# Dilated attention on one core: both slots of a pair per step in two row tiles, scores in full float without a split, values turned once in the projection

## The reference, cut to what matters

```python
q, k, v = parts of h @ w_in                     # q: 3 groups x 8 slots x 64; k, v: 8 slots x 64
for g, (window, dilation) in enumerate(((128, 1), (512, 4), (2048, 16))):
    # tokens by residue t % dilation; blocks of 128 queries against 256 keys (their own block and the one before)
    scores = (q_block @ k_blocks.T) * 64 ** -0.5, masked to 0 <= distance <= 128
    m = max(scores); p = exp(scores - m); den = sum(p)
    o[g] = (p @ v_blocks) / den;  lse[g] = m + log(den)
out = sum over g of softmax(lse)[g] * o[g]
y_attn = out * silu(g_attn)
```

## Time and profile before

| | us |
|---|---|
| median of 3 runs | 2815.51 (2813.55 to 2815.75) |
| the profiled execution | 2818.68 |
| its span | 2817.1 |
| PE busy | 2741.9 (97%) |
| PE weight loads | 2262.5 (80%) |
| DVE busy | 1591.9 (57%) |
| ACT busy | 1238.4 (44%) |
| POOL busy | 1573.7 (56%) |

### The profile page before, as it was taken

One profiled execution on the slowest core, in us unless ns is written; L12 is line 12 of the kernel. 1 busy time (PEld: TensorE's weight loads), 2 busy tenths in 40 slices (PEclk: granted clock), 3 DMA queues, 4 the chain that ended last, 5 costly groups with the idle time before them and its releaser, 6 DMA issues. The chain is left out here.

```text
span 2817.1 us, 45199 instructions
## 1 busy us (share of the span) xinstructions
PE 2741.9 (97%) x16510; PEld 2262.5 (80%) x16510; DVE 1591.9 (57%) x2527; ACT 1238.4 (44%) x2258; POOL 1573.7 (56%) x1078
## 2 busy tenths in 40 slices
PE   6999999999999999999999999999999999999998
PEld 5888888888887788888887777777999877788787
DVE  6335324797544345885534556565777786743433
ACT  5232233433234444332233655656777854532332
POOL 7777778877776788777774545544111354232000
PEclk8999999999999999999999999999999999999999
DMA  3557435532225255332135655545676578954543
GB/s 127 141 176 214 137 117 153 146 111 96 67 90 194 90 160 156 105 113 82 55 110 172 190 161 185 185 158 184 204 211 192 146 243 271 300 171 149 179 141 112
DMA packets 462813, 436.24 MB, mean 155 GB/s; under 512 B 60736, under 2 KB 403008, under 8 KB 454976
## 3 DMA queue, kind: packets, MB, share of 16 engines
q1 hardware_dynamic: 460352, 425.79, 48.8%
q0 software_dynamic: 2304, 8.39, 0.8%
HBM read 290.99 MB, written 143.13 MB: 154 GB/s over the span
## 5 line engine op out<-in xcount | busy, mean ns | idle before, releaser
L552 PE MATMUL p_acc<-h_kept,w_hi 128*128 128x512 f32 x1216 | 475.7, 391 | 4.6 <-ACT work L598 3.1
L554 PE MATMUL p_acc<-h_kept,w_lo 128*128 128x512 f32 x1216 | 474.1, 390 | 0.0
L553 PE MATMUL p_acc<-h_kept,w_hi 128*128 128x512 f32 x1216 | 474.1, 390 | 0.0
L433 POOL TENSOR_TENSOR w_lo<-p_sums,w_hi 128x512 fp32r<-128x512 f32 x300 | 387.2, 1307 | 131.8 <-ACT w_hi L639 131.8
L639 ACT ACTIVATE w_hi<-p_sums 128x512 fp32r<-128x512 f32 x300 | 189.2, 632 | 472.6 <-PE p_acc L554 447.9
L552 PEld LDWEIGHTS p_acc<-h_kept,w_hi 128*128 128x128 f32 x1216 | 228.8, 188 | 54.4 <-ACT work L598 3.3
L554 PEld LDWEIGHTS p_acc<-h_kept,w_lo 128*128 128x128 f32 x1216 | 228.8, 188 | 47.8
L553 PEld LDWEIGHTS p_acc<-h_kept,w_hi 128*128 128x128 f32 x1216 | 228.9, 188 | 47.0
L552 PE MATMUL p_acc<-p_ops,w_hi 128*128 128x512 f32 x608 | 238.0, 391 | 7.1 <-DVE p_ops L740 7.1
L553 PE MATMUL p_acc<-p_ops,w_hi 128*128 128x512 f32 x608 | 237.3, 390 | 0.0
L554 PE MATMUL p_acc<-p_ops,w_lo 128*128 128x512 f32 x608 | 237.3, 390 | 0.0
(11 more groups left out here) (344 smaller groups left out, 6686.7 us busy)
## 6 DMA issues: line engine op xcount, KB each, us to landing
raw<-w_in SPq DMA_DIRECT2D x100, 512.0 KB, 4.7
s_qs<-p_stage SPq DMA_DIRECT2D x96, 256.0 KB, 4.0
work<-s_gates SPq DMA_DIRECT2D x48, 512.0 KB, 7.3
p_rawb<-w_in SPq DMA_DIRECT2D x38, 512.0 KB, 3.7
keep<-w_in SPq DMA_DIRECT2D x38, 512.0 KB, 4.8
s_xbc<-p_stage SPq DMA_DIRECT2D x32, 512.0 KB, 2.6
work<-s_xbc SPq DMA_DIRECT2D x16, 1024.0 KB, 6.3
spare<-s_qs SPq DMA_DIRECT2D x16, 1024.0 KB, 7.9
```

The lines of the kernel that those rows point to most:

```text
L433: tt(w_lo[:, k], weight(u, k), w_hi[:, k], ALU.subtract).then_inc(w_made, 1)
L552: pe.matmul(bank, hi, ops[k][:, 0, c], start=c == 0, stop=False)
L553: pe.matmul(bank, hi, ops[k][:, 1, c], start=False, stop=False)
L554: last = pe.matmul(bank, lo, ops[k][:, 0, c], start=False, stop=c == 3)
```

## The change

The projection has kinds "k" and "v" in place of "kv", in the order of the sets (in the second half after "g", values ahead of keys). Queries aren't split: `sum_out` writes them, reordered by residues, into the stage buffer, and one DMA per tile stores 128 rows, both slots. Values are turned after the third product of the next set, by transposes of 64 rows in two row tiles, ACT copies them to the stage buffer, and SP stores them tokens by channels. Keys aren't split in the attention stage. A step of attention is one block in both slots: the slots' 64 rows are two row tiles (`tile_position` (0, 0) and (64, 0)), the score is one float32 matmul per slot over 64 rows. Probabilities are turned in row tiles, two steps (a "duo") at a time; ACT copies the upper rows' half and DVE the lower rows' half of every duo. Values come by DMA straight in the order of the pattern, nine DMAs per pair, in pieces of 512 bytes. The ones for the sums of probabilities stand at both ends of the pair's 130 columns. The merge stage reads the changed layout.

```diff
-FIRST_HALF = (("gates", 12), ("kv", 4), ("g", 2), ("q", 6), ("xbc", 8), ("sc", 8), ("z", 4))
-SECOND_HALF = (("z", 4), ("q", 6), ("xbc", 8), ("sc", 8), ("g", 2), ("kv", 4))
+FIRST_HALF = (("gates", 12), ("k", 2), ("v", 2), ("g", 2), ("q", 6), ("xbc", 8), ("sc", 8), ("z", 4))
+SECOND_HALF = (("z", 4), ("q", 6), ("xbc", 8), ("sc", 8), ("g", 2), ("v", 2), ("k", 2))
...
+            r = PATTERNS[(2 * i + m) // 4][1] if kind == "q" else 1
+            if r > 1:
+                ordered = lambda ap: ap.rearrange("p (m r) -> p m r", r=r)
+                whole = stage[:, u % 2 * 2 + m].rearrange("p (r m) -> p m r", r=r)
+                to, a, b = whole[:, n * BANK // r:(n + 1) * BANK // r], ordered(a), ordered(b)
             return dve.tensor_tensor(to, a, b, ALU.add)
...
+                        if k == 3 and u and SETS[u - 1][0] == "v":
+                            pe.wait_ge(posted, before(u - 1, posted_by_act))
+                            pe.wait_ge(post_made, before(u - 1, posted_by_dve))
+                            pe.wait_ge(h_made, 8)
+                            for m in range(2):
+                                banks = [conv[m][:, r * BANK:(r + 1) * BANK].rearrange("p (b q) -> p b q", q=HDIM) for r in range(2)]
+                                for b in range(TILES // 2):
+                                    last = transpose_by_rows(pe, [bank_of_r[:, b] for bank_of_r in banks],
+                                                             stage[:, (u - 1) % 2 * 2 + m, b * P:(b + 1) * P], ident)
+                                last.then_inc(v_turned, 1)
...
+            @block.tensor
+                def score(j):
+                    ...
+                    if j >= 2:
+                        pe.wait_ge(masked, j - 1)
+                    for sl in range(2):
+                        rows = slice(sl * HDIM, (sl + 1) * HDIM)
+                        last = pe.matmul(ps_s[:, j % 2, sl, 2 * P - n:2 * P], q_s[g][rows, b * P:(b + 1) * P],
+                                         keys_of(k_s[pair][rows], g, r, (m + 1) * P - n, n), start=True, stop=True,
+                                         tile_position=(sl * HDIM, 0))
+                def turn(duo):
+                    pe.wait_ge(exped, 2 * duo + 2)
+                    if duo:
+                        for rows in range(2):
+                            pe.wait_ge(t_taken[rows], duo)
+                    for e in range(2):
+                        for sl in range(2):
+                            for h in range(2 - width(g, b + e) // P, 2):
+                                last = transpose_by_rows(pe, [ps_t[:, rows, sl, 2 * e + h] for rows in range(2)],
+                                                         probs[:, (2 * duo + e) % 4, sl, h * P:(h + 1) * P], ident)
+                for duo in range(DUOS + OUT_LAG):
+                    if duo < DUOS:
+                        score(2 * duo)
+                        score(2 * duo + 1)
+                    if TURN_LAG <= duo < DUOS + TURN_LAG:
+                        turn(duo - TURN_LAG)
+                    if duo >= OUT_LAG:
+                        output(duo - OUT_LAG)
...
+                # DVE
+                for duo in range(DUOS + OUT_LAG + 1):
+                    if duo > OUT_LAG:
+                        take(duo - OUT_LAG - 1)
+                    if duo < DUOS:
+                        mask(2 * duo)
+                        mask(2 * duo + 1)
+                    if TURN_LAG <= duo < DUOS + TURN_LAG:
+                        evacuate(dve, 1, dve.tensor_copy, duo - TURN_LAG)
```

More of the change, by code:

```diff
@@ L798, in finish @@
                     done = before(u, posted_by_dve)
[L799 to L807 removed]
+                    if kind == "xbc":
                         convolve(u, 0, (1, 0))
@@ L973, in projection_stage @@
         s.clear()
-def load_keys(sp, d, k_raw, pair, sl, loaded):
-    for half in range(2):
-        sp.dma_start(k_raw[HDIM * half:HDIM * (half + 1)], d["kv"][pair, HDIM * sl:HDIM * (sl + 1)]).then_inc(loaded, 16)
 def ssd_gates_stage(nc, w, d, h, wt, v, ident, eps, spare, keep, first):
@@ new lines, in output @@
+                def output(duo):
+                    pair, g, b = place(duo)
+                    if b == 0:
+                        pe.wait_ge(v_loaded[g], 16 * v_loads[g] * (pair + 1))
+                    for rows in range(2):
+                        pe.wait_ge(t_taken[rows], duo + 1)
+                    if duo >= 2:
+                        pe.wait_ge(o_taken, duo - 1)
+                    for e in range(2):
+                        for sl in range(2):
+                            first_h = 2 - width(g, b + e) // P
+                            for h in range(first_h, 2):
+                                last = matmul_by_columns(pe, ps_o[:, duo % 2, 2 * e + sl, :OUT_W],
+                                                         probs_t[:, duo % 2, sl, 2 * e + h],
+                                                         v_tok[:, g, b + e - 1 + h, sl * OUT_W:(sl + 1) * OUT_W],
+                                                         start=h == first_h, stop=h == 1)
+                    last.then_inc(o_made, 1)
@@ new lines, in mask @@
+                def mask(j):
+                    pair, (g, b) = j // NS, steps[j % NS]
+                    if b == 0:
+                        dve.wait_ge(stored[g], 16 * stores[g] * (pair + 1))
+                    if j >= 4:
+                        dve.wait_ge(exped, j - 3)
+                    dve.wait_ge(s_made, j + 1)
+                    n = width(g, b)
+                    for sl in range(2):
+                        last = dve.tensor_tensor_reduce(
+                            out=scores[:, j % 4, sl, 2 * P - n:], in0=ps_s[:, j % 2, sl, 2 * P - n:2 * P],
+                            in1=bands[g][:, 2 * P - n:], scale=-HDIM ** -0.5, scalar=-NEG, op0=ALU.add, op1=ALU.min,
+                            accum_out=att[g][:, b, 2 * OUT_W + sl:2 * OUT_W + sl + 1])
+                    last.then_inc(masked, 1)
```

473 lines of the change are left out of this document (158 added, 315 removed).

## The result

The changed kernel takes 2768.26 us (median of 4 runs, 2762.34 to 2772.98) against 2815.15 for the kernel before (4 runs beside it): a ratio of 0.9833, 95% interval 0.9813 to 0.9853, so 47 us less. Forecast were 2751, 65 us less than before, and a range of 2735 to 2782. The profiled execution took 2769.81 us, its span is 2768.2 against 2817.1.

The account below looks back on a forecast made before the run. TensorE, busy 97%, was taken as the bound. Attention falls from 283.6 to 214 us (-69.6: four pairs 210, ends 4), projection +5, sum -65: profiled 2818.68 becomes 2754, median 2751; range 2735 to 2782.

Parts of the forecast that it names:

- Full-float products in row tiles run side by side: Attention scores: two row tiles' full-float records overlap, 0.216 us per wide record pair and 0.11 per narrow; no row showed it.
- Rival 2: Attention scores: full-float row-tile products don't overlap, +0.87, +0.66, +0.44 us a duo; kernel time 2807 us; chance 4%.
- rival 3: Attention scores: row-tile products one after the other with weight loads in the open; stage 352, kernel time 2889 us; chance 3%.
- Wide duo 2.59: Attention duo of 256-key blocks: TensorE sets the pace, 2.59 us.
- Mixed 2.03: Attention duo of one narrow (128-key) and one wide (256-key) block: a draw of TensorE and VectorE, 2.03 to 2.06 us.
- Narrow 1.72 by VectorE: Attention duo of 128-key blocks: VectorE sets the pace at 1.72 us, not TensorE at 1.46.
- Tiling changes 0.29 per duo: TensorE in each attention duo: 0.29 us for changes of tiling, kept as before.
- Ends 4: Attention stage's ends: late values, handing-over copies, filling and draining the loop; together 0 to 8 us, taken as 4.
- Values at the start covered or up to 4 late: Attention start: nine value loads ahead of the first output, about 5 us of scores before it; covered or up to 4 us late.
- Projection +5: Projection: four sets of values turn 16 blocks each in row tiles, 4 x 1.25 = +5 us, bounds 4 and 8.
- Values stored after ACT's late copy: Projection: SP's value stores wait behind the next raw load, already issued; nothing on TensorE's path.
- Rival 1: Attention: VectorE bounds every duo, 2.82, 2.46, 2.12 us; 60.3 a pair, 245 with ends, kernel time 2782 us; chance 15%.

Follow-up runs that it names:

- run 6: Changed kernel with both slots' scores on the same 64 rows of the array, so they cannot run side by side; 2884.57 us in one execution.
- run 1: Changed kernel with the third group's scores reading the first 128 keys in one piece instead of 16-byte steps (other keys); 2766.43 us, ratio 0.9822.
- run 5: Changed kernel with probabilities turned on the whole array, one transpose per block, instead of in two row tiles; 2801.68 us, ratio 0.9947.
- run 8: Changed kernel with values' sets ahead of the gate's sets in the projection's second half, attention stage untouched; 2766.31 us, ratio 0.984.
- run 4: Changed kernel without values, queries or fourth keys loaded after the first pair, outputs stored only behind the last pair; 2778.53 us in one execution, stage 225.75.
- run 3: Changed kernel with queries loaded for the first pair only and the fourth pair using the second's keys; 2766.67 us, ratio 0.9834.
- run 2: Changed kernel with values loaded for the first pair only, later pairs reusing them; 2764.56 us, ratio 0.9821.

## Why the prediction was right, and where it was off

The kernel became faster, in the forecast's way and within its range; the forecast was 17 us too low. That it came so near owes something to luck: the attention stage alone missed by 24.6 us, and in the profiled executions 9 us of that came back in the scan and the merge stage, which the forecast put at 0, and 2.9 in front of the first score. By its own steps:

- **TensorE bounds the stage:** right. VectorE waited for scores, 4.2 us in 14 waits over the 58 us of the second pair, and TensorE never waited over 0.3 us for it in the whole stage.
- **Full-float products in row tiles run side by side** (the one price without a row, taken as 0.216 per wide pair): right, shown by the timeline and by run 6. Rival 2 is out, and with it rival 3.
- **Wide duo 2.59:** 2.64. **Mixed 2.03, alternating with wide:** 2.31 and 2.41, a mean of 2.36 where (2.03 + 2.59)/2 is 2.31. **Narrow 1.72 by VectorE:** 1.93 by TensorE. This is the mis-sized term. "0.11 narrow" for a score record came from rows whose operand lies in one run, and I carried it to a group that reads keys at steps of 16 bytes; there it is 0.22. The two errors partly cancelled, as VectorE needs only 1.5 (run 1): its copies follow each other after 0.34 us, and I had taken their duration, 0.42. The sum of a pair: 54.95 for 52.5, four pairs +10 us. The pattern stood in `keys_of` before, and the earlier trace rows are of this very group (its queries lie in `a_q`), but there it had no price that could be seen: the split products of 128 strided columns follow each other after 0.11 us, as the transposes of 128 columns do. Only the full-float product shows it.
- **Tiling changes 0.29 per duo:** 0.34, as what the wide duo's 2.64 has over its 0.87, 0.50 and 0.93; run 5 gives 0.15 for one more.
- **Ends 4:** 6.
- **Nothing for the loading of instructions:** this step was missing, 13 us. I had counted instructions as time only, not as bytes that reach TensorE through the DMA engines. The window of the earlier trace rows had a DMA share of 0.72, and the change makes the stage denser and the values' pieces 512 bytes, so both were there to be read; that "the DMA volume of a pair hardly moves" was true of the bytes and not of the pieces, which over the stage went from 31408 packets of q1 to 54804. Together with the third group it is all of the stage's 25 us (238.6 against 214).
- **Values at the start covered or up to 4 late:** covered; no output waited for them. The 2.9 us ahead of the first score were gained because 16 value turns stood there before, after a wait for their order. In their place TensorE now waits for GpSimd's ones. I had counted the turns but not the wait.
- **Projection +5:** +5.3, and by its parts: the four sets behind which values are turned take 20.41 us from start to start where their neighbours take 19.04 (20.2 and 19.0 forecast), and those with queries stay at 19.04.
- **Values stored after ACT's late copy: "nothing on PE's path":** wrong by 2.5. I named the next raw load as issued already, but not the load behind it, of the block with which the gates start. Run 8 wins back 0.7 to 1.8 of it; the rest stays open.
- **Merge and scan 0:** not contradicted, by the second trace of before; up to 7 us of the medians' 47 aren't placed.
- **Rival 1, VectorE everywhere (241 with 60.3 per pair):** the stage's 238.6 look like it, but by another way: duos are 2.64, not 2.82, and the missing time is idle TensorE with VectorE idle too. Only the duo's parts and the waits tell the two apart; the stage's sum doesn't.

**What stays open:** why a load of code comes late only in some of the crowded stretches. The places aren't chance: run 8, with the same attention stage, has its eight pauses in the same duos as eight of the ten above (every changed kernel but those of runs 5 and 6 has one in the seventh duo of the first pair's second group: 0.46 us in the quiet run 4, 1.96 to 2.93 us in the others), and only their lengths and two further ones differ. What sets the place wasn't tested, and no run here changed how the instruction queue stands among the others. Whether the number of pieces, the bytes or the time of the DMA engines decides isn't shown either.

## What to carry to other kernels

When a change makes TensorE's stream denser with many small instructions, count them as traffic too: 16 KB per some 244 matmuls and weight loads, which must get through beside the kernel's own transfers, and look for "issue" waits where the DMA share is near 1, with a load of the instruction queue landing just before they end. Take the same stage in two executions before comparing pauses: here they differed by 3.6 of 11.4 us. Price a matmul by rows with the same address pattern of its operand, not only the same shape; an operand in steps of 16 bytes halves the pace, and an idle engine can put it in order beforehand. When a stage's time fits a rival's sum, compare the steps before taking the rival for confirmed.

## What the runs showed of the hardware beyond that

- TensorE can stand 0.4 to 2.9 us with nothing awaited, until a 16 KB load of its instructions lands, and goes on 1.3 to 1.5 us after that; ten times in 240 us here, never in the stage with 600 fewer matmuls (run 5), nor in 110 us with the queues nearly empty (run 4). The load itself takes about as long with full queues as with nearly empty ones (medians 1.03 and 1.00 us); it starts late.
- About as many bytes in pieces of 512 bytes keep the DMA engines busy for longer than in pieces of 8 KB: 9.00 MB at 64.7% in run 3, 9.53 MB at 55.3% in run 2, over 55 us.
- A full-float score of 128 columns: 0.11 us per pair of tiles from keys in one run, 0.22 from keys in steps of 16 bytes.
- Three tilings in a duo instead of two cost 0.15 us more.
- With the scores on half of the rows only, the granted clock fell to 0.50 at the start of each pair, for 20 to 31 us (run 6), with TensorE busy all the while. The changed kernel has both halves at work and kept 0.99 over the stage; its share of 0.50 is 3.4 us twice. That the idle half of the rows is the reason isn't shown by this one run.
